# Two chained layer stacks on one core: first weight cast earlier, identity transposes ahead of the input, step-size chain later, last output block in two token parts

## The reference

```
h = ssd_mixer(x);  x = layer_norm(alpha*x + h)      # in-projection, causal conv, SSD scan, gate, norm, out-projection
h = dsa_mixer(x);  x = layer_norm(alpha*x + h)      # low-rank q/kv, top-k index scores, attention, gate, out-projection
x = x + gmlp_branch(rms_norm(x))                    # u, v, gate; per-group token mixing; out-projection
x = x + stick_breaking_branch(rms_norm(x))          # q, k, v, gate; stick-breaking attention; out-projection
out = rms_norm(x, final_g)                          # [1, 256, 2048]
```

## Time and profile before

| | |
|---|---|
| time, median of 3 (range) | 2460.84 us (2459.45 to 2461.24) |
| the profiled execution | time 2461.91 us, span 2460.2 us |
| PE busy | 2435.3 us (99%) |
| DVE, ACT, POOL busy | 1566.9 us (64%), 1236.3 us (50%), 92.9 us (4%) |
| DMA | 459.53 MB, mean 187 GB/s; 59.2% of the 16 engines' time |
| first product with a weight | 11.19 us |
| last matmul ends | about 2449.99 us |
| span ends | 2460.2 us |

### The profile page before, as it was taken

One profiled execution on the slowest core, in us unless ns is written; L12 is line 12 of the kernel. 1 busy time (PEld: TensorE's weight loads), 2 busy tenths in 40 slices (PEclk: granted clock), 3 DMA queues, 4 the chain that ended last, 5 costly groups with the idle time before them and its releaser, 6 DMA issues.

```text
span 2460.2 us, 45395 instructions
## 1 busy us (share of the span) xinstructions
PE 2435.3 (99%) x19640; PEld 2344.6 (95%) x19640; DVE 1566.9 (64%) x2097; ACT 1236.3 (50%) x1415; POOL 92.9 (4%) x70
## 2 busy tenths in 40 slices
PE   8999999999999999999999999999999999999998
PEld 7999999999999999999988899999999999999998
DVE  5768887866577776665575556656555555555556
ACT  4445666554454565554464445445444445455453
POOL 0001100010022000000000000000000000000002
PEclk9999999999999999999999999999999999999999
DMA  6766666557755655446756666666655565555544
GB/s 178 231 197 187 191 197 189 180 172 234 236 172 175 197 155 163 152 149 235 228 179 188 190 187 194 193 184 190 184 189 189 189 196 172 175 171 170 186 156 172
DMA packets 264840, 459.53 MB, mean 187 GB/s; under 512 B 18667, under 2 KB 69953, under 8 KB 262721
## 3 DMA queue, kind: packets, MB, share of 16 engines
q1 hardware_dynamic: 264641, 456.63, 59.2%
HBM read 452.18 MB, written 4.26 MB: 186 GB/s over the span
## 4 chain that ended last, share of the span: by engine, by line
PE 96%; DVE 1%; DMA 1%; ACT 1%; issue 1%; SPq 0%; POOL 0%; ACTq 0%
PE G L678 89%; PE M L678 5%; PE M L691 1%; DMA WS<-in_a_w_s 0%; DVE W L1494 0%; DMA XS<-in_x 0%; ACT W L1085 0%; DVE BT L1533 0%; DMA RAW<-in_ssd_w_in 0%; DVE WY L1494 0%; DVE W0m L1494 0%; DVE W2m L1494 0%; DVE E L1586 0%; ACT RES L1475 0%; ACT W2m L1085 0%
## 5 line engine op out<-in xcount | busy, mean ns | idle before, releaser
L678 PE MATMUL G<-AA,W 128*128 128x256 f32 x7884 | 942.1, 278 | 5.8 <-DVE W L1494 5.7
L678 PEld LDWEIGHTS G<-AA,W 128*128 128x128 f32 x7884 | 916.9, 188 | 12.7 <-DVE W L1494 6.7
L1494 DVE TENSOR_TENSOR W<-RAW,W 128x1024 fp32r<-128x1024 f32 x431 | 539.3, 1253 | 366.6 <-ACT W L1085 364.9
L1085 ACT CAST W<-RAW 128x1024 fp32r<-128x1024 f32 x431 | 449.0, 1046 | 469.1 <-PE G L678 454.9
L678 PE MATMUL G<-AA,WY 128*128 128x256 f32 x2532 | 308.7, 278 | 0.0
L678 PEld LDWEIGHTS G<-AA,WY 128*128 128x128 f32 x2532 | 296.7, 188 | 2.6 <-issue 2.2
L1494 DVE TENSOR_TENSOR WY<-RAW,WY 128x1024 fp32r<-128x1024 f32 (+1 forms) x127 | 159.3, 1256 | 89.3 <-ACT WY L1085 89.3
L678 PE MATMUL G<-W,AA 128*128 128x512 f32 x864 | 205.7, 394 | 0.0
L678 PEld LDWEIGHTS G<-W,AA 128*128 128x128 f32 x864 | 161.3, 187 | 39.6
L678 PE MATMUL G<-W2m,YY 128*128 128x256 f32 x1536 | 186.6, 276 | 1.0 <-DVE W2m L1494 1.0
L678 PE MATMUL G<-W1m,YY 128*128 128x256 f32 x1536 | 185.7, 276 | 0.1
(11 more groups left out here) (289 smaller groups left out, 2338.2 us busy)
## 6 DMA issues: line engine op xcount, KB each, us to landing
RAW<-in_a_w_in SPq DMA_DIRECT2D x192, 512.0 KB, 3.7
RAW<-in_ssd_w_in SPq DMA_DIRECT2D x160, 512.0 KB, 4.4
RAW<-in_b_w_in SPq DMA_DIRECT2D x128, 512.0 KB, 4.0
RAW<-in_dsa_w_in SPq DMA_DIRECT2D x72, 512.0 KB, 3.5
RAW<-in_ssd_w_out SPq DMA_DIRECT2D x64, 512.0 KB, 4.8
RAW<-in_dsa_w_out SPq DMA_DIRECT2D x64, 512.0 KB, 4.2
RAW<-in_a_w_out SPq DMA_DIRECT2D x64, 512.0 KB, 3.5
RAW<-in_b_w_out SPq DMA_DIRECT2D x32, 512.0 KB, 3.8
```

Source lines behind the costliest of these rows:

```text
L678: return e.matmul(o, l, r, start=start, stop=stop, skip_group_check=True)
L1085: e.copy(wh[:, 0:n], RAW[:, v % NR, 0:n]).then_inc(*up(cast_done, "cast", v))
L1494: e.tensor_tensor(wl[:, 0:n], RAW[:, v % NR, 0:n], wh[:, 0:n].bitcast(F), ALU.subtract).then_inc(*up(rest_done, "rest", v))
```

## The change

It has six parts.

1. **First weight unit cast ahead.** In `slots`, slot 0 alone is free at unit 0, and slots 1 and 2 come free at units 1 and 2. In `turn_in` ACT and DVE yield once more, after tiles 0 and 1: they now do tiles 0 and 1, unit 0, tiles 2 and 3, unit 1 and so on. PE keeps its order.
2. **Identity transposes.** PE does 8 transposes of `ident` ahead of the wait for the first part of x and 10 ahead of the second, into PSUM bank 3, which nobody reads.
3. **Step-size chain.** SP's store of `cs` moves 8 ticks later, ACT's exp and ln 2 later, DVE's second half 1 later, PE's transposes 1 later.
4. **Last column block of the third layer.** For `ev_o3(4)` the transposes, the rounding and the rest each come one tick later.
5. **Last block in two parts.** `("o4", 4)` joins `HALVED` with its 4 units, and two slots `WC` are added from the units 0 and 2 of `("o4", 3)` on.
6. **The finish.** It runs once for each half of the tokens, the first behind the first pass. For each half: add, squares, sum, root, reciprocal; then ACT scales columns 0 to 767, DVE 768 to 1791, and DVE scales the last 256 and multiplies them by `final_g` in one instruction (POOL did that multiplication before). SP stores 3 pieces for each half, in place of 2.

```diff
-HALVED = {("o1", 4): (4, 8), ("cq", 0): (0, 4), ("o2", 4): (4, 8), ("v5", 0): (0, 4)}
+HALVED = {("o1", 4): (4, 8), ("cq", 0): (0, 4), ("o2", 4): (4, 8), ("v5", 0): (0, 4), ("o4", 4): (0, 4)}
+OUT_COLS = ((0, 768), (768, 1024), (1792, 256))
 # Plan.slots
+        for i in range(2):
+            extra[f"c{i}"] = (self.blocks["o4", 3][2 * i], len(self.units))
-        free = [(i, None) for i in range(3)]
+        free = [(0, None)]
         for u, t in self.steps:
+            if 0 < u < 3:
+                free.insert(0, (u, None))
 # walk
-        for j in range(2, 5):
+        for j in range(2, 4):
             run(("o4", j), ("ev_o4", j))
-        drain()
-        start("finish")
+        twice(("o4", 4), None, ("finish",))
         drain()
 # SP
         def dt_task():
+            for _ in range(8):
+                yield
             e.wait_ge(*on("dt", "cs"))
...
-            for q in range(2):
-                for t in range(2):
-                    e.wait_ge(*on("final", q, t))
-                    e.dma_start(out[0, t * P:(t + 1) * P, 1024 * q:1024 * q + 1024],
+            for t in range(2):
+                for i, (c, w) in enumerate(OUT_COLS):
+                    e.wait_ge(*on("final", t, i))
+                    e.dma_start(out[0, t * P:(t + 1) * P, c:c + w], OUT[:, t, c:c + w]).then_inc(
 # PE
         def turn_in():
             e.wait_ge(*on("ident"))
             for k in range(0, 16, 2):
+                if k < 4:
+                    for _ in range(8 + k):
+                        transpose(M[:, 3, 0:P], ident[:, :], ident[:, :])
         def dt_task():
-            for _ in range(5):
+            for _ in range(6):
                 yield
         def ev_o3(i):
             c, w = LAST_COLS[i]
             yield
+            if i == 4:
+                yield
 # ACT
         def turn_in():
-                if k % 4 == 2:
+                if k % 4 == 2 or k == 0:
                     yield
         def dt_task():
             e.activation(nea, alog[:, :], ACT.Exp).then_inc(*up(act_made, "nea"))
+            yield
+            yield
             e.wait_ge(*on("dt", "abs"))
         def ev_o3(i):
...
+            if i == 4:
+                yield
             for f in range(w // P):
         def finish():
+            c, w = OUT_COLS[0]
+            for t in range(2):
+                e.wait_ge(*on("ssum", t))
+                e.activation(RR[:, t:t + 1], RR[:, t:t + 1], ACT.Sqrt, scale=1.0 / DM, bias=eps6[:, 0:1]).then_inc(
+                    *up(act_made, "sroot", t))
+                e.wait_ge(*on("srec", t))
+                e.wait_ge(*on("fg", 3, 1))
+                o = OUT[:, t, c:c + w]
+                e.activation(o, o, ACT.Copy, scale=RR[:, t:t + 1]).then_inc(*up(act_made, "final", t, 0))
 # DVE
         def turn_in():
-                if k % 4 == 2:
+                if k % 4 == 2 or k == 0:
                     yield
         def dt_task():
...
+            yield
             yield
             yield
             e.wait_ge(*on("dt", "ln"))
         def ev_o3(i):
...
+            if i == 4:
+                yield
         def finish():
+            b = ("o4", 4)
+            e.wait_ge(*on("sqrt_in"))
+            for t in range(2):
+                e.wait_ge(*(done(b) if t else on("half", b)))
+                add8(4, t)
+                e.wait_ge(*on("sq8", 4, t))
+                e.tensor_reduce(RR[:, t:t + 1], SS[:, t, :], AX.X, ALU.add).then_inc(*up(dve_made, "ssum", t))
+                e.wait_ge(*on("sroot", t))
+                e.reciprocal(RR[:, t:t + 1], RR[:, t:t + 1]).then_inc(*up(dve_made, "srec", t))
+                e.wait_ge(*on("srec", t))
+                e.wait_ge(*on("fg", 3, 1))
+                c, w = OUT_COLS[1]
                 o = OUT[:, t, c:c + w]
+                e.tensor_scalar(o, o, RR[:, t:t + 1], None, ALU.mult).then_inc(*up(dve_made, "final", t, 1))
+                c, w = OUT_COLS[2]
+                o = OUT[:, t, c:c + w]
+                e.scalar_tensor_tensor(out=o, in0=o, scalar=RR[:, t:t + 1], in1=FG[:, c:c + w], op0=ALU.mult,
+                                       op1=ALU.mult).then_inc(*up(dve_made, "final", t, 2))
```

More of the change, by code:

```diff
@@ L320, in program @@
                                   ("SS8", [P, 2, 5], F), ("RR8", [P, 2], F)])
+    WC = spare("WC", 2, s_at + 8 * DM + 4 * DM + 2560)
     QI = QKB[:, 1]
@@ L337, in pair_of @@
             return w[:, 0:UW], w[:, UW:2 * UW]
-        if s[0] in "ab":
-            w = (WA if s[0] == "a" else WB)[int(s[1])]
+        if s[0] in "abc":
+            w = {"a": WA, "b": WB, "c": WC}[s[0]][int(s[1])]
             return w[:, 0:UW], w[:, UW:2 * UW]
@@ L657, in finish @@
         def finish():
-            for q in range(2):
-                for t in range(2):
-                    e.wait_ge(*on("final", q, t))
-                    e.dma_start(out[0, t * P:(t + 1) * P, 1024 * q:1024 * q + 1024],
-                                OUT[:, t, 1024 * q:1024 * q + 1024]).then_inc(*landed(d["out_stored"], "stored"))
+            for t in range(2):
+                for i, (c, w) in enumerate(OUT_COLS):
+                    e.wait_ge(*on("final", t, i))
+                    e.dma_start(out[0, t * P:(t + 1) * P, c:c + w], OUT[:, t, c:c + w]).then_inc(
+                        *landed(d["out_stored"], "stored"))
             e.wait_ge(*on("stored"))
@@ L1081, in unit @@
                     e.wait_ge(*on("end3", "pe"))
+                elif str(plan.slot[v])[0] == "c":
+                    e.wait_ge(*on("end7", "dve"))
+                    e.wait_ge(*on("end7", "act"))
+                    e.wait_ge(*on("end7", "pe"))
                 elif plan.slot[v] == "x7":
@@ L2197, in set8, with add8 @@
             yield
+        def add8(j, t):
+            c, w = LAST_COLS[j]
+            o = OUT[:, t, c:c + w]
+            e.tensor_tensor(o, o, g_of(("o4", j))[:, 512 * t:512 * t + w], ALU.add).then_inc(
+                *up(dve_made, "sum8", j, t))
+            e.wait_ge(*on("sum8", j, t))
+            if j or t:
+                e.wait_ge(*(on("sq8", j, 0) if t else on("sq8", j - 1, 1)))
+            e.tensor_tensor_reduce(out=TT[:, 0:w], in0=o, in1=o, scale=1.0, scalar=0.0, op0=ALU.mult,
+                                   op1=ALU.add, accum_out=SS[:, t, j:j + 1]).then_inc(
+                                       *up(dve_made, "sq8", j, t))
         def ev_o4(j):
             b = ("o4", j)
-            c, w = LAST_COLS[j]
             e.wait_ge(*done(b))
             for t in range(2):
[L2204 to L2212, removed]
+                add8(j, t)
             here(dve_made, "g_read", b)
@@ L2216, in finish @@
         def finish():
-            e.wait_ge(*on("sq8", 4, 1))
+            b = ("o4", 4)
             e.wait_ge(*on("sqrt_in"))
[L2219 to L2227, removed]
+            for t in range(2):
[8 more added lines that the diff above has]
+                c, w = OUT_COLS[1]
+                o = OUT[:, t, c:c + w]
+                e.tensor_scalar(o, o, RR[:, t:t + 1], None, ALU.mult).then_inc(*up(dve_made, "final", t, 1))
+                c, w = OUT_COLS[2]
+                o = OUT[:, t, c:c + w]
+                e.scalar_tensor_tensor(out=o, in0=o, scalar=RR[:, t:t + 1], in1=FG[:, c:c + w], op0=ALU.mult,
+                                       op1=ALU.mult).then_inc(*up(dve_made, "final", t, 2))
             yield
```

## The result

The changed kernel takes 2447.57 us (median of 4 runs, 2446.83 to 2447.94) where the kernel before takes 2460.51 in the same sitting: the ratio is 0.9946, with a 95% interval of 0.9934 to 0.9958. That is 12.9 us faster; 14.3 us were forecast, to 2446.5, in a range of 2443.9 to 2450.5. A second sitting of the same kernel gave 2446.40 (5 runs) against 2460.18, 13.8 us, ratio 0.9944 (0.9932 to 0.9957).

What follows compares the result with a forecast made beforehand. PE bounds the kernel, busy 2435.3 of 2460.2 us, so only its idle or half-clock stretches can be won. 4.5 + 5.4 + 0.9 + 3.5 = 14.3 us off, to a median of 2446.5, range 2443.9 to 2450.5.

Steps and rivals of the forecast that it cites:

- The start: First 28 us: earlier first cast and a clock raised by transposes bring unit 4 forward; 4.5 us, bounds 2.3 to 5.2.
- The cast: Start: unit 0's cast stood behind the second tiles in ACT's order, not its weight; unit 0 starts 2.3 us earlier.
- The late weight unit 4: Start: weight unit 4, landing at 19.9, is late next; PE waits 0.7 us, then unit 4 starts at 23.4.
- rival 1: Start: transposes don't raise the clock, unit 0 stays slow; start gives 2.3 to 3.2 us, total 2448.2; chance 0.29.
- The clock: Start: 18 added transposes raise the clock before unit 0, which takes 2.7 instead of about 5.2; a further 2.5 us.
- The step sizes: Stretch 50 to 72 us: PE's 2.29 us wait, the half clock behind it and late fetches go; 5.4 us, bounds 3.0 to 5.6.
- The third layer: Its last block: PE's wait for DVE's add is covered by the next block's first unit; 0.9 us, bounds 0.5 to 1.0.
- The tail: Last block and finish: first half's finish and stores run under the second pass; 3.5 us, bounds 2.2 to 4.3.
- Rival 2: Step sizes: unit 12's rest comes late, the stall partly stays, 3 to 5 us of 5.4 gone; 2450.5; chance 0.08.
- Rival 3: Weight supply: earlier PE drains the buffers sooner, up to the start's 4.5 us lost again; 2451; chance 0.07.
- Rival 4: Last block: fourth weight late, PE idles, second pass at half clock, slower than before; 2461 with 9 us idle; chance 0.02.
- Rival 5: Whole kernel: no change, all the gains lie off the path; chance 0.04.

Runs made afterwards that it cites:

- experiment 2: The kernel before with the 18 identity transposes alone; ratio 1.0000 (0.9991 to 1.0009), 2461.25 us against 2460.88.
- experiment 3: The kernel before with both the earlier first cast and the identity transposes; ratio 0.9985 (0.9976 to 0.9994), 2457.03 us against 2460.88.
- experiment 7: The changed kernel run again with nothing altered; 2446.40 us.
- experiment 9: The changed kernel without its 18 identity transposes; 2448.29 us against 2446.40.
- experiment 1: The kernel before with the earlier first cast alone (slots and extra yields), no identity transposes; ratio 0.9990 (0.9981 to 0.9999), 2457.86 us against 2460.88.
- experiment 4: The kernel before with the step-size chain moved alone, on all four engines; ratio 0.9977 (0.9968 to 0.9985), 2455.09 us against 2460.88.
- experiment 10: The kernel before with the last block in two passes, spare slots and the finish by halves; ratio 0.9986 (0.9977 to 0.9995), 2456.82 us against 2460.18.
- experiment 12: The kernel before with the third layer's last tiles one unit later, alone; ratio 0.9996 (0.9988 to 1.0005), 2459.24 us against 2460.28.
- experiment 11: The changed kernel with the last block's units in one pass, the finish still by halves; 2449.69 us.
- experiment 5: The kernel before with SP's store of the running sums 8 ticks later, alone; ratio 0.9992 (0.9984 to 1.0001), 2458.45 us against 2460.28.
- experiment 6: The changed kernel with ACT's exponential and logarithm back at their old tick; 2449.77 us, ratio to the kernel before 0.9961 (0.9947 to 0.9974).

## Why the prediction was right, step by step

**The start, 4.5 us forecast; 4.5 by the one pair of traces, about 4 by all of them.** The cast waited for ACT's order and not for its weight: so it was, and it started at 6.16 (6.55 reckoned). Transposes raise the clock: so it is (experiments 2, 3, 7, 9). The late weight unit 4 as the next limit: found, with 0.4 us of wait where 0.7 was reckoned. The split between the two sources was off, and the two errors nearly cancel, which is luck. The cast was put at 2.3 us and gives 2.8 (experiments 1 and 9 against the mean of the old starts, inside rival 1's 2.3 to 3.2). The clock was put at what remains of 4.5, 2.2 us, and gives 1.2 to 1.3 behind the early cast (24.60 and 24.74 against 23.4): a unit 0 without the transposes takes 4.70 and 5.25 us there and not the 5.39 of the trace that was read, and the wait in front of the vectors' transposes, which only the faster start meets, takes back 0.2 to 0.7 us in four of the five traces.

**The step sizes, 5.4 forecast, 5.4 measured** (experiment 4). The attribution was right too: ACT's stand at the exponential is 4.1 of it, SP's store 1.2; the text had put 0.6 in two small waits on the store, which is their idle alone. What it had wrong in the detail is the half clock as a fixed price of the idle. Eight traces have the idle of 2.29 us; in seven the clock fell behind it, and in experiment 3 it stayed up, and the time was lost at the fetches instead. In that trace the start's edits give 3.4 us by CB, where they give 4.5 between experiment 4 and the changed kernel. The medians show no such dependence within their scatter: 3.85 (experiment 3), 5.79 (4), 3.36 (10) and 1.04 us (12) are 14.0 together, and all at once gave 12.9 and 13.8.

**The third layer, 0.9 forecast, 1.0 measured. The tail, 3.5 forecast, 3.4 measured;** its mechanism, half of the finish and half of 2 MB under the second pass, is shown by experiment 11 (2.8 of 3.4 us). DVE's squares take 0.42 us with POOL idle and 0.72 beside its multiplication, as was read. The prediction had the second half's first store 2.7 us behind the last matmul; it is issued at 2442.22, 2.6 behind it.

**The sum.** With the start at 4.0 to 4.1 the four terms are 13.8 to 13.9, and the second sitting had 13.8; the first had 12.9, and the intervals don't tell the two apart. The forecast lies 1.1 us under the first sitting's median for a reason that can be named in part. It took the profiled execution before, 2461.91, 1.1 us above its kernel's median, and carried this distance over to the changed kernel. But half a microsecond of it is the slow start of that one trace, which the change removes, and the changed kernel's profiled execution, forecast at 2447.6 and measured at 2447.86, lies only 0.3 above its median. That the forecast came within 0.3 us of the profiled execution is luck in part: 1.6 us lost at the `CSB` load in the trace after stand against 1.0 of `WS` waits in the trace before.

**The rivals.** Rival 1, a clock that transposes don't raise, is refuted: in experiment 2 PE has done nothing but transposes when the second tiles take 0.60 us in place of 1.12, and unit 0 runs in 3.0 us in all six traces that have them and the early cast, against 4.70 and 5.25 in the two with the cast alone. The Trainium skill (TensorE: Matmul & The Clock Gate, Part 4: PE-mode transpose) says that transpose mode doesn't count as busy for the clock; here the measurement decides against it for these float32 transposes, the second ten taking 1.51 us where the first eight took 1.97. Rival 2, a rest late at unit 12: its slack is 0.9 us, and none of the six traces with the moved chain has a wait there. Rival 3 didn't occur in the changed kernel, but a form of it did in experiment 3. Rival 4: 2.3 us of slack at the fourth weight, no wait. Rival 5: the ratio's interval ends at 0.9958.

## What to carry to other kernels

Before pricing a wait, ask whether the engine in front waited for data or for its own program order: a cast that starts 2.3 us after its data landed is a gain without any cost, and an ACT instruction waiting on DVE costs what is queued behind it, not its own 0.42 us. Filling PE's idle to raise the clock pays only if the following gap is closed as well (the transposes gave nothing by themselves in experiment 2's median, and were worth 1.2 to 1.3 us behind the early cast). Before a difference between two traces is taken as the gain, look at the same stretch in other traces that share it: the start of the kernel before varies by 1.1 us from one to the next, half as much as the clock's part was forecast to give. At the end of a kernel whose result can't be scaled before the last sum, splitting the last block by rows and not by columns hides half of the finish and of the stores under matmuls (2.8 us of 10.2 here).

## What the runs showed of the hardware

The clock's response isn't the same from run to run. In the same kernel it rose near 5 us in one run and after the second tiles, between 7.9 and 8.5 us, in the next (ten transposes in 1.51 and in 2.34 us). The idle of 2.29 us ahead of unit 12 brought the half clock in seven traces of eight (the kernel before and experiments 1, 2, 5, 6, 10 and 12), with a unit of 24 matmuls at 4.22 to 4.64 us, and didn't in experiment 3 (3.02 us), where the clock fell only behind a second idle of 2.1 us. An idle of 2.88 us behind transposes brought it too (0.57 and 0.50 granted, 4.55 us for the unit in experiment 2); an idle of 1.0 us in the changed kernel did not (3.03 us).

Small loads scatter more than the differences under test: one of eight equal loads took 11.0 us to land where the median is 8.5, and that alone cost PE 1.8 us at the end of a chain of four engines' steps.

The granted clock of the records reads 1.00 in the first 16 us of 13 of the 14 traces, though the length of the matmuls halves within that time; there only the durations tell. The exception is experiment 2, where the clock rose, fell and rose again: its first fall, near 10 us, is the first thing that the granted clock shows.
